# An encoder trunk with a mixture of experts: another expert is fetched ahead of the routing, and the first job gathers for its successor later

## The reference

```python
def moe_swiglu(x, router_w, router_b, wg, wu, wd):
    logits = xt.astype(F32) @ router_w.astype(F32) + router_b.astype(F32)
    top_logit, top_idx = lax.top_k(logits, TOP_K)          # TOP_K = 2 of N_EXPERTS = 8
    top_w = jax.nn.softmax(top_logit, axis=-1)
...
    def expert_block(args):
        tok, w, e = args
        xb = xt[tok]
        h = jax.nn.silu(xb @ wg[e]) * (xb @ wu[e])
        return (h @ wd[e]).astype(F32) * w[:, None]
```

## Time and profile before

| | |
|---|---|
| median of 3 runs | 1170.74 us (1169.42 to 1171.97) |
| profiled execution | 1171.44 us |
| its span | 1169.0 us |
| TensorE busy | 1126.1 us, 96% |
| VectorE busy | 669.3 us, 57% |
| ScalarE busy | 542.4 us, 46% |
| GpSimd busy | 77.9 us, 7% |
| moved by DMA | 377.88 MB, 323 GB/s on average |

### The profile page before, as it was taken

One profiled execution on the slowest core, in us unless ns is written; L12 is line 12 of the kernel. 1 busy time (PEld: TensorE's weight loads), 2 busy tenths in 40 slices (PEclk: granted clock), 3 DMA queues, 4 the chain that ended last, 5 costly groups with the idle time before them and its releaser, 6 DMA issues.

```text
span 1169.0 us, 16635 instructions
## 1 busy us (share of the span) xinstructions
PE 1126.1 (96%) x6525; PEld 834.4 (71%) x6525; DVE 669.3 (57%) x934; ACT 542.4 (46%) x840; POOL 77.9 (7%) x101
## 2 busy tenths in 40 slices
PE   8998999999999998999999999999999999999995
PEld 7976888887897887855688755688755788655441
DVE  6788545455777897810698710898610998411104
ACT  4774444444486675610676610776401876301002
POOL 0001000001000396000000000000000000000001
PEclk8998999999999999999999999999999999999998
DMA  9833554554434198989999999999899999899994
GB/s 385 358 131 145 227 204 171 200 182 144 165 115 181 75 371 339 365 348 421 421 421 420 380 405 420 420 422 421 356 422 420 420 421 420 353 422 420 421 420 176
DMA packets 52764, 377.88 MB, mean 323 GB/s; under 512 B 5888, under 2 KB 6016, under 8 KB 7120
## 3 DMA queue, kind: packets, MB, share of 16 engines
q1 hardware_dynamic: 51408, 370.69, 78.7%
q0 software_dynamic: 992, 5.56, 1.3%
q10 hardware_dynamic: 288, 0.59, 0.1%
HBM read 375.77 MB, written 1.05 MB: 322 GB/s over the span
## 4 chain that ended last, share of the span: by engine, by line
PE 78%; DVE 7%; DMA 5%; ACT 4%; POOL 4%; issue 1%; DVEq 0%; ACTq 0%; SPq 0%; POOLq 0%
PE bank L813 15%; PE bank L563 11%; PE bank L565 11%; PE bank L564 10%; PE bank L804 7%; PE bank L715 5%; PE bank L718 5%; PE bank L721 5%; DMA raw<-W 4%; PE bank L790 3%; DVE wlo L1592 2%; PE bank L736 1%; PE bank L557 1%; PE bank L875 1%; PE bank L795 1%
## 5 line engine op out<-in xcount | busy, mean ns | idle before, releaser
L1592 DVE TENSOR_TENSOR wlo<-raw,whi 128x1024 fp32r<-128x1024 f32 x260 | 305.5, 1229 | 18.6 <-ACT whi L1145 17.7
L1145 ACT ACTIVATE whi<-raw 128x1024 fp32r<-128x1024 f32 x260 | 255.4, 1051 | 0.0
L565 PE MATMUL bank<-whi,al 128*128 128x512 f32 (+1 forms) x624 | 235.1, 377 | 0.0
L813 PE MATMUL bank<-raw,xg 128*64 128x256 f32 x1760 | 205.4, 383 | 2.8 <-DMA raw<-W 2.6
L1644 DVE TENSOR_TENSOR he<-he,bank 128x128 f32<-128x128 f32 x55 | 15.8, 288 | 289.3 <-ACT he L1200 289.3
L813 PEld LDWEIGHTS bank<-raw,xg 128*64 128x64 f32 x1760 | 120.2, 137 | 67.8 <-DMA raw<-W 6.1
L1270 DVE TENSOR_TENSOR wlo<-raw,whi 128x1024 fp32r<-128x1024 f32 x110 | 130.4, 1222 | 27.7 <-ACT whi L964 26.9
L563 PE MATMUL bank<-whi,xgh 128*128 128x512 f32 x352 | 142.7, 405 | 2.7 <-DVE wlo L1592 2.5
L564 PE MATMUL bank<-wlo,xgh 128*128 128x512 f32 x352 | 137.1, 390 | 0.0
L565 PEld LDWEIGHTS bank<-whi,al 128*128 128x128 f32 x624 | 118.8, 190 | 22.2
L964 ACT ACTIVATE whi<-raw 128x1024 fp32r<-128x1024 f32 x114 | 115.3, 1057 | 23.3 <-PE bank L565 17.5
(11 more groups left out here) (285 smaller groups left out, 1434.0 us busy)
## 6 DMA issues: line engine op xcount, KB each, us to landing
raw<-W SPq DMA_DIRECT2D x352, 1024.0 KB, 12.2
scr<-gb_d POOLq DMA_DIRECT2D x3, 1024.0 KB, 5.1
scr<-wbd_d POOLq DMA_DIRECT2D x2, 512.0 KB, 6.2
x<-gb_d POOLq DMA_DIRECT2D x1, 1024.0 KB, 8.2
out_d<-acc SPq DMA_DIRECT2D x4, 256.0 KB, 2.0
x<-x_d SPq DMA_DIRECT2D x1, 512.0 KB, 4.0
x<-x_d ACTq DMA_DIRECT2D x1, 512.0 KB, 8.7
rtab<-rt_d POOLq DMA_DIRECT2D x1, 228.0 KB, 2.8
```

The lines of the kernel that those rows point to most:

```text
L565: return nc.tensor.matmul(out, sl, mh, start=False, stop=last, skip_group_check=True)
L813: last = nc.tensor.matmul(bank[n * NARROW:(n + 1) * NARROW, c % 2, 0:FC].rearrange("p (a n) -> p a n", a=2), xg[:, kk, :], gu[:, :, n * P: ...
L1145: nc.scalar.activation(whi[:, q % SPLIT, h * HW:(h + 1) * HW], raw[:, i % RING, h * HW:(h + 1) * HW], ACT.Copy).then_inc(hi_rdy, 1)
L1592: V.tensor_tensor(wlo[:, q % SPLIT, h * HW:(h + 1) * HW], raw[:, i % RING, h * HW:(h + 1) * HW], whi[:, q % SPLIT, h * HW:(h + 1) * HW].bi ...
```

## The change

The expert chosen beforehand is the last (7) and no longer the first (0): its weights are fetched as the first job's, its key gets the 1.0e5, and its places make the first one-hot matrix. In the first job the one-hot matrix for the second is made at step 22 and no longer at 14, and the two halves of the gather come behind steps 25 and 28 and no longer behind 17 and 20. All other jobs are as before.

```diff
+FIRST = NE - 1
+FIRST_S_AT = 22
+FIRST_GATHER_AFTER = {25: 0, 28: 1}
...
                 if m < FFP:
-                    sp.dma_start(raw[:, s, :], W[STREAM + m]).then_inc(raw_in[s], 16)
+                    sp.dma_start(raw[:, s, :], W[STREAM + FIRST * FFP + m]).then_inc(raw_in[s], 16)
...
-                link(G.tensor_scalar(key[:, 0:1], key[:, 0:1], 1.0e5, None, ALU.add))
+                link(G.tensor_scalar(key[:, FIRST:FIRST + 1], key[:, FIRST:FIRST + 1], 1.0e5, None, ALU.add))
...
-                if i in GATHER_AFTER:
+                halves = FIRST_GATHER_AFTER if first else GATHER_AFTER
+                if i in halves:
                     if not first:
                         pe.wait_ge(acc_rdy, J * 4)
                     pe.wait_ge(S_rdy, J + 2)
-                    gather(GATHER_AFTER[i], WIDE if wide_after else NARROW)
+                    gather(halves[i], WIDE if wide_after else NARROW)
...
-                    if i == S_AT:
+                    if i == (FIRST_S_AT if first else S_AT):
                         dve.wait_ge(st_ps, J + 1)
                         dve.wait_ge(tab_rdy, 1)
                         one_hot([ps_[:, t, J + 1:J + 2] for t in range(NT)], NARROW)
...
-            one_hot([ps_e[:, t, 0:1] for t in range(NT)], WIDE)
+            one_hot([ps_e[:, t, FIRST:FIRST + 1] for t in range(NT)], WIDE)
```

## The result

The changed kernel takes 1091.13 us (median of 4 runs, 1090.63 to 1091.76) beside 1170.33 us for the kernel before: ratio 0.9322, 95% interval 0.9306 to 0.9338. The profiled execution took 1091.76 us with a span of 1089.9. The forecast was 1089.8 us with a range of 1087 to 1094. So the time lies inside it. One term of the forecast, the jump over the loop taken as 0, was off by 3.3 us; part of that is hidden in the total, because the first job began 0.9 us earlier in this profile for a reason the change does not touch. The end of the program went as the rival *jump* said.

What follows compares the result with a forecast made beforehand. TensorE sets the pace, nearly balanced with DMA, over nine expert jobs end to end. 1171.44 - 76.9 (extra job) - 4.4 (stall) = 1090.1 us, put down as 1089.8 on the median's footing; range 1087 to 1094, forecast case 1087.5 to 1091.5.

Steps and rivals of the forecast that it cites:

- the jump over the loop: Before the tail, engines newly branch over the skipped loop; taken as 0, up to 3.6 us kept for the range.
- rival *jump: Before the tail, code behind the skipped loop must be fetched, 1.5 to 3.6 us uncovered, taken as 3: 1093.1; chance 0.20.
- The extra job: After the eighth job: with expert 7 forced, no token is left over and the run-time loop's pass vanishes, 76.9 us less.
- The stall: First job: VectorE's wait at step 14 for GpSimd's table goes away, giving TensorE 4.4 us of VectorE's 5.0.
- the cover: At the loop's end, time between an engine's branch and its next work: 1.9 us on ScalarE, 2.2 us on TensorE.
- the two ends: Bounds for the jump's cost: nothing, or 5.5 us, the landing of a small DMA, if code must be fetched.
- The tables: First job: GpSimd at 1.03 us a step writes the places by 454.7, before VectorE reaches step 22 at 463.5; no wait.
- the list of jobs: First job: SyncE's weight queue wants it at about 461, GpSimd writes it at 460.9: a tie, costed at 0.
- such a delay is made up: Weight ring: with 11 pieces loaded or coming, a microsecond's lateness is recovered before the first narrow job, costing 0.

Runs made afterwards that it cites:

- part2_alone: Changed kernel with expert 0 chosen first again, keeping only the later one-hot matrix and gathers of the first job; 1164.37 us, ratio 0.9948.
- part1_alone: Changed kernel with the first job's one-hot matrix back at step 14, gathers behind 17 and 20; expert 7 still first; 1097.66 us, ratio 0.9381.
- tail_first: Changed kernel with TensorE's last scatter also ahead of the loop, run there when no extra job exists; 1088.24 us, ratio 0.9294.
- no_loop_pe: Changed kernel with TensorE's loop over extra jobs and its branch left out, other engines' loops kept; 1088.13 us, ratio 0.9289.
- short_loop_pe: Changed kernel with only 3 of 33 steps in the body of TensorE's skipped loop, jump still taken; 1087.25 us, ratio 0.9285.
- first_is_4: Changed kernel with expert 4 (57 tokens, the smallest) chosen beforehand in place of 7; 1164.61 us, one run.

## Why the prediction was right, and where not

**The extra job (76.9 us).** Right in cause and nearly in size. The step from counts to jobs held for four choices of the first expert (0 and 4 give an extra job, 7 and 3 give none). Between `part2_alone`, which has the extra job, and the changed kernel, which has not, the time from the first SiLU of the first job to ScalarE's first step of the tail falls from 743.8 us (1146.99 - 403.16) to 667.7 (1071.07 - 403.38), by 76.1 us. Not all of this reaches the end: it is 73.2 us in the medians (1164.37 - 1091.13), because the tail grew.

**The stall (4.4 us).** Right in cause, a little small. In the traces the first job is 4.5 us shorter than before and 5.0 us shorter than in `part1_alone`: TensorE took over nearly the whole wait of VectorE. The way I read it, one long step less a normal one with a gather, gives 4.8 us in `part1_alone`.

**The jump (taken as 0).** This is the step that failed. I had the cover right (2.2 us on TensorE) and the two ends, 0 and 5.5 us, and chose the lower end although the upper one was the only row I had. The branch takes 3.8 us, and 1.9 us are left uncovered: the scatter begins 2.67 us behind ScalarE's copy and not 0.74. What I had not priced at all is what follows a gap on TensorE: its clock fell to 1.2 GHz during the scatter, and the tail grew by 1.4 us more, 3.3 us in all (18.8 against 15.5 from ScalarE's copy to the end). `tail_first`, `no_loop_pe` and `short_loop_pe` take the gap away, each in another way, and with it the clock stays at 1.00 through the scatter and the 3.3 us return. That the 1.4 us are the clock's is shown by the traces in which it fell later behind the same gap. The rival "jump" had the right mechanism, and I gave it 0.20. That its price of 3 us is close to the 3.3 us is luck: it stood for uncovered time alone, which is 1.9 us. It is also the case that the Trainium skill spoke for ("Runtime: NRT & Kernel Launch", Instruction fetch mechanics: a taken branch outside the window fetches its page first), and by this rule, 3.4 to 3.9 us for 33 or 16 steps and 0.25 us for 3, the traces agree.

**Why the sum still fitted.** The forecast put ScalarE's copy at 1076.5 - 4.4 = 1072.1; it came at 1071.07. Of these 1.1 us, 0.9 are the start of the first job (first SiLU shown at 403.38 against 404.29), in a stretch that the change does not touch and that scatters between profiles. From the first SiLU to ScalarE's copy the trace is 81.5 us shorter (749.2 against 667.7), and 76.9 + 4.4 = 81.3 us were forecast: the two terms that I did price are right to 0.2 us. So -1.1 and +3.3 make 2.2 us: 1087.7 us of span were forecast, 1089.9 measured. The time lies in the forecast's own range of 1087.5 to 1091.5, but the end of the program went the way of the rival. That the total is so near is in part the luck of that earlier start.

**The tables.** The chain of GpSimd was forecast to end its second L482 (now L485) at 454.7 and the list of jobs (now L493) at 460.9 if it kept to 1.03 us a step. It did, nearly (53 steps from 399.31 to 454.48, 1.04 us each; it also began 0.9 us earlier than before):

```profile
453.24 1.24 POOL L485 TENSOR_TENSOR msc<-tabs 128x17 f32<-128x17 f32 x1
...
459.94 1.07 POOL L493 CAST jobs_i<-tabs 128x17 int32<-128x17 f32 x1
```

They end at 454.5 and 461.0. VectorE came to step 22 at 461.2 and waited for nothing; 6.7 us were to spare where I had 9, since its steps took 2.74 us and not 2.90. But the list of jobs was late, where I had a tie. The waits of SyncE's queue from 400 to 500 us:

```profile
SPq L376 <- POOL jobs_i L493: 5.1, 1, 5.1
```

I had taken 4.4 to 5.0 us off the old time of 465.6 and forgotten that a gather of 1.8 us, which used to lie ahead of that point, is moved behind it too. The piece whose slot is wanted is split by 458.5 (the first two of VectorE's four L1596 from 456.11), and the list could be loaded at 461.1 only, so it was 2.6 us late. It cost nothing, for the reason given: the pieces in the ring lasted, and TensorE has no wait on a weight DMA in the whole of the changed kernel. The forecast that such a delay is made up held.

## What to carry to other kernels

Where the work depends on data, count the jobs in the trace (instructions of a group, DMAs of a line) before counting microseconds: here one token over a limit of 64 was worth 6.5% of the time (76.1 of 1170 us), and the gain of this change holds only for inputs in which the forced expert is among the large ones and nothing is then left over. Where a run-time loop is usually skipped, put the usual path straight behind the test and the skipped body last; a far jump on the engine that sets the end has to be priced. When a move of one step is costed by shifting old times, shift by everything that moved past the point, not by the stall alone.

## What the runs showed of the hardware

- A taken branch on TensorE over a loop body of 16 or 33 steps took 3.4 to 3.9 us in its queue, over one of 3 steps 0.25 us, and 0.08 to 0.09 us where it was not taken. ScalarE's and VectorE's jumps over their much shorter bodies (27 and 23 instructions in the window of the extra job, beside TensorE's 495 matmuls) took 0.05 and 0.07 us.
- TensorE's queue came to the register load behind a job 2.1 to 2.2 us before the array had finished the matmuls ahead of it, and to the branch 1.3 us before, and no sooner when 4.7 us of matmuls more were put there.
- After 2.3 to 2.75 us of idle TensorE the granted clock fell from 1.00 to 0.50 while it worked again, 0.8 to 2.6 us into the scatter, in seven traces of seven; after 0.78 us in one of six (`first_is_4`, 2.7 us into it).
- GpSimd's steps on tables of 1 to 136 columns went at 1.03 us each on average beside a busy VectorE (39 in 40 us), and 14 of them took 4.95 us while it stood still.
